# Seven block products of half-size matrices for the second half of an output projection's columns

## The reference

```python
hn   = rmsnorm(x, pre_gain)
q, k, v, g_a, u, g_b = split(hn @ w_in)          # 2048 -> 6 x 1024
y_a  = stick_breaking(q, k, v) * silu(g_a)       # 8 heads x 128
y_b  = multiscale_pool(u, w_pool) * silu(g_b)    # 4 groups x 256
mix  = concat(y_a, y_b)                          # 512 x 2048
out  = mix @ w_out                               # 2048 -> 2048
x    = x + rmsnorm(out, post_gain)               # norm over a token's 2048 columns
```

## Time and profile before

| | us |
|---|---|
| median of 3 runs | 749.54 (749.45 to 750.86) |
| profiled execution | 749.17 |
| its span | 747.4 |
| TensorE busy | 726.2 (97%), 3792 matmuls |
| VectorE busy | 527.9 (71%) |
| ScalarE busy | 406.0 (54%) |
| GpSimd busy | 62.8 (8%) |

### The profile page before, as it was taken

How to read it: one execution, slowest core, us unless ns; L and a number is a source line. 1 busy time by engine, 2 the same in 40 slices (tenths; PEclk the granted TensorE clock), 3 DMA queues, 4 the chain that set the end, 5 groups by cost and what they waited for, 6 DMA issues and landing times.

```text
span 747.4 us, 9753 instructions
## 1 busy us (share of the span) xinstructions
PE 726.2 (97%) x3792; PEld 618.4 (83%) x3792; DVE 527.9 (71%) x661; ACT 406.0 (54%) x538; POOL 62.8 (8%) x85
## 2 busy tenths in 40 slices
PE   6999989999999999999999999999999999999995
PEld 4778868888888888888888888888877888888884
DVE  3499978888788888788888987897978532133323
ACT  4754566666666656766657666756676232222200
POOL 0000000110020110020110011110000000000000
PEclk9999999999999999999999999999999999999998
DMA  8955445676646666746756656666644613053143
GB/s 288 390 152 129 139 109 146 168 176 171 173 107 178 170 165 182 175 114 169 193 147 169 173 150 170 169 148 163 181 140 172 225 62 138 26 169 102 67 142 112
DMA packets 36237, 118.08 MB, mean 158 GB/s; under 512 B 4064, under 2 KB 5088, under 8 KB 35552
## 3 DMA queue, kind: packets, MB, share of 16 engines
q1 hardware_dynamic: 30288, 96.49, 38.9%
q0 software_dynamic: 5760, 20.97, 16.5%
q10 hardware_dynamic: 144, 0.01, 0.0%
HBM read 113.26 MB, written 4.19 MB: 157 GB/s over the span
## 4 chain that ended last, share of the span: by engine, by line
PE 79%; DVE 9%; ACT 4%; issue 3%; DMA 2%; SPq 1%; POOL 0%; DVEq 0%; POOLq 0%; ACTq 0%
PE ps L1361 33%; PE ps L1363 17%; PE ps L1301 9%; PE ps L1300 9%; PE ps L1299 9%; DMA x_rows<-x 2%; DVE raw_lo L830 2%; DVE mix L867 1%; PE ps L1391 1%; PE ps L1389 1%; ACT w_hi L486 1%; DVE a_ops L899 1%; DVE a_ops L897 1%; DVE a_ops L1082 1%; SPq L381 0%
## 5 line engine op out<-in xcount | busy, mean ns | idle before, releaser
L1361 PE MATMUL ps<-a_ops,w_hi 128*128 128x512 f32 x1120 | 397.9, 399 | 3.6 <-ACT p_neg L584 1.6
L1363 PE MATMUL ps<-a_ops,raw_lo 128*128 128x256 f32 x1120 | 314.2, 281 | 0.0
L1361 PEld LDWEIGHTS ps<-a_ops,w_hi 128*128 128x128 f32 x1120 | 210.5, 188 | 55.8 <-DVE raw_lo L830 2.5
L830 DVE TENSOR_TENSOR raw_lo<-raw,w_hi 128x1024 fp32r<-128x1024 f32 x155 | 188.2, 1219 | 34.7 <-ACT w_hi L486 33.9
L1363 PEld LDWEIGHTS ps<-a_ops,raw_lo 128*128 128x128 f32 x1120 | 211.5, 189 | 0.3
L486 ACT ACTIVATE w_hi<-raw 128x1024 fp32r<-128x1024 f32 x155 | 163.3, 1055 | 66.4 <-PE ps L1363 62.9
L1299 PE MATMUL ps<-a_ops 128*128 128x512 f32 x192 | 75.0, 391 | 1.4 <-DVE a_ops L1082 1.1
L1300 PE MATMUL ps<-a_ops 128*128 128x512 f32 x192 | 74.8, 390 | 0.0
L1301 PE MATMUL ps<-a_ops 128*128 128x512 f32 x192 | 74.7, 389 | 0.0
L1270 POOL DMA_DIRECT2D raw<-w_heads x40 | 34.9, 871 | 308.4 <-DMA raw<-w_heads 308.4
L1090 DVE TENSOR_TENSOR a_ops<-raw,a_ops 128x1024 fp32r<-128x1024 f32 x24 | 28.3, 1219 | 37.8 <-ACT a_ops L682 37.8
(11 more groups left out here) (147 smaller groups left out, 919.5 us busy)
## 6 DMA issues: line engine op xcount, KB each, us to landing
raw<-w_heads SPq DMA_DIRECT2D x100, 512.0 KB, 4.9
raw<-w_heads POOLq DMA_DIRECT2D x40, 512.0 KB, 7.3
raw<-w_out SPq DMA_DIRECT2D x32, 512.0 KB, 4.5
raw<-w_v SPq DMA_DIRECT2D x15, 512.0 KB, 10.1
mix<-xT SPq DMA_DIRECT2D x16, 256.0 KB, 9.9
x_rows<-x SPq DMA_DIRECT2D x4, 1024.0 KB, 12.5
raw<-x SPq DMA_DIRECT2D x8, 512.0 KB, 5.2
out<-mix SPq DMA_DIRECT2D x6, 512.0 KB, 2.7
```

The costliest lines, as they stand in the source:

```text
L830: dve.tensor_tensor(raw_slot(raw_lo, slot), raw_slot(raw, slot), hi_slot(g).bitcast(F32), ALU.subtract).then_inc(w_split, 1)
L1361: pe.matmul(dst, hi[:, w], a_ops[:, a:a + SEQ], start=k == 0 and p in (0, 1, 5), stop=False, skip_group_check=True)
L1363: mm = pe.matmul(dst[:, HALF:SEQ], lo[:, w], a_ops[:, a:a + HALF], start=False, stop=k == KH - 1, skip_group_check=True)
```

## The change

The dc 0 quarter stays. The dc 1 quarter is computed with the same matmuls, but in eight "plain" steps of half a chunk (24 matmuls each) whose weights are rounded into the three slots of `w_hi` and subtracted into ten slots (`late_slot`), where the chunks had slots of their own. The two last quarters, dc 2 and 3 together, become one block product: tokens in halves of 256, inner dimension in halves of 1024, columns in halves of 512, and seven products of halves in place of eight. A product is 4 steps (q) of 2 inner tiles x 2 row tiles x 3 = 12 matmuls. The order of the steps is the list `LATE`. Weight t + 2 is rounded once step t - 1 is through (`late_hi_of` waits for `late_done >= t`).

For this, four operands of the mix tiles are new: three sums (`s_sums`, `s4_sums`, split by `s_hi_of`, `s_lo_of` into the places of the first three weight chunks) and one difference (split by `s3_hi_of`, `s3_lo_of` in place of mix parts that the plain steps have used). Of the weights, products 1 and 4 want the sum of two blocks (a load and an adding DMA by GpSimd, `add_late`), products 2 and 6 a sum of VectorE's (`late_sum`). The results are put together by ScalarE's copies out of PSUM (`keep_of`) and VectorE's sums (`join_e2`, `join_f`, `join_g`, `join_second`, `join_c12`). Rows 2 and 3 are complete after step 28 (of 0 to 35), rows 0 and 1 only behind the last two steps. The gain rows are loaded behind chunk 3 instead of before chunk 0. The rows are finished in the order 2, 3, 0, 1, and row 1 has the four pieces. Each square now waits for the one before it, since they share one scratch tile. In one tile (row 0, dc 3) the first token, whose mix is zero, is multiplied by 0 (`not_first`).

```diff
+PAIRS = KH // 2
+LATE = [("plain", q) for q in range(2 * PAIRS)]
+LATE += [(p, q) for q in range(PAIRS) for p in (0, 1, 2, 6)]
+LATE += [(3, 0)] + [(4, q) for q in range(PAIRS)] + [(3, q) for q in range(1, PAIRS)]
+LATE += [(5, q) for q in range(PAIRS)]
+LATE_STEPS = len(LATE)
+LATE_SLOTS = 10
+LATE_OF = {kind: t for t, kind in enumerate(LATE)}
+FORM = 2 * PAIRS
+ROW_ORDER = (2, 3, 0, 1)
+TAIL_ROWS = (0, 1)
...
+        FORM_BANK = {0: ACC, 5: ACC, 1: ACC + 2, 3: ACC + 2, 2: 0, 4: 0, 6: 2}
...
+        FORM_TILES = ((2, 2), (2, 3), (3, 2), (3, 3), (0, 3), (1, 3), (0, 2), (1, 2))
...
@@ SyncE
+            sp.wait_ge(o_chunk_done, KK)
             sp.dma_start(post_gain_rows[:, :],
                          post_gain.partition_broadcast(P)).then_inc(rows_gain_loaded, 16)
-            for j in range(RAW_SLOTS, OUT_HALVES + RAW_SLOTS):
-                sp.wait_ge(o_split, j - RAW_SLOTS + 1)
-                load_half(j)
+            load_late(RAW_SLOTS)
+            load_late(RAW_SLOTS + 1)
+            sp.wait_ge(s_split, 3 * PAIRS)
+            load_late(RAW_SLOTS + 2)
+            for t in range(LATE_SLOTS, LATE_STEPS + 2 * TT):
+                sp.wait_ge(late_done, t - LATE_SLOTS + 1)
+                load_late(t)
@@ ScalarE
+            for q in range(PAIRS):
+                s_hi_of(q, 1)
+                s_hi_of(q, 2)
+            for q in range(PAIRS):
+                s_hi_of(q, 3)
+                if q < 2:
+                    late_hi_of(q)
+            for t in range(LATE_STEPS - 2):
+                late_hi_of(t + 2)
+                if t == 0:
                     for s in range(TT):
-                        rows_square(s, n // KK)
+                        rows_square(s, 0)
+                if PAIRS <= t < 2 * PAIRS:
+                    s3_hi_of(t - PAIRS)
+                if t == FORM:
+                    for s in range(TT):
+                        rows_square(s, 1)
+                if t == LATE_OF[0, PAIRS - 1] + 1:
+                    keep_of(0, 0)
+                    keep_of(0, 1)
+                if t == LATE_OF[1, PAIRS - 1] + 1:
+                    keep_of(1, 0)
+                    keep_of(1, 1)
+                if t == LATE_OF[4, PAIRS - 1] + 1:
+                    for n in range(4):
+                        rows_square(*FORM_TILES[n])
+            for n in range(4, 8):
+                rows_square(*FORM_TILES[n])
@@ VectorE
+            for q in range(PAIRS):
+                s_sums(q)
+                s_lo_of(q, 1)
+                s_lo_of(q, 2)
+            for q in range(PAIRS):
+                s4_sums(q)
+                s_lo_of(q, 3)
+                if q < 2:
+                    late_lo_of(q)
             dve.wait_ge(rows_gain_loaded, 16)
+            for t in range(LATE_STEPS - 2):
+                if LATE[t + 2][0] == 1:
+                    late_sum(2, LATE[t + 2][1])
+                if LATE[t + 2][0] == 2:
+                    late_sum(6, LATE[t + 2][1])
+                late_lo_of(t + 2)
...
+                if t == LATE_OF[2, PAIRS - 1] + 1:
+                    join_e2(0)
+                    join_e2(1)
+                if t == LATE_OF[6, PAIRS - 1] + 1:
+                    join_f(0)
+                    join_f(1)
+                    join_g(0)
+                    join_g(1)
+                if t == LATE_OF[4, PAIRS - 1] + 1:
+                    join_second(0)
+                    join_second(1)
+                if t == LATE_OF[4, PAIRS - 1] + 2:
+                    for n in range(4):
+                        rows_gain(*FORM_TILES[n])
+                if t == LATE_OF[4, PAIRS - 1] + 3:
+                    row_mean(2)
+                    row_mean(3)
+                if t == LATE_OF[3, PAIRS - 1] + 1:
+                    join_c12(0)
+                    join_c12(1)
...
+            row_final(2)
+            for i in range(2):
+                rows_gain(i, 3)
+            row_final(3)
+            for n, s in enumerate(TAIL_ROWS):
...
+                rows_gain(s, 2)
+                row_final(s)
@@ GpSimd
+            for q in range(PAIRS):
+                add_late(1, q)
+            for q in range(PAIRS):
+                add_late(4, q)
@@ TensorE
+            def form_tile(t, i):
+                p, q = LATE[t]
+                for k in range(2):
+                    mm = three(form_bank(p, i), form_operand(p, 2 * q + k, i), late_weights(t, k),
+                               p in (0, 1, 2, 4, 6) and q == 0 and k == 0,
+                               p in (3, 4, 5, 6) and q == PAIRS - 1 and k == 1)
+                return mm
...
+            for t in range(FORM):
+                plain_step(t)
+            for t in range(FORM, LATE_STEPS - 2):
+                form_step(t)
+            t = LATE_STEPS - 2
+            pe.wait_ge(late_split, t + 1)
+            form_tile(t, 0)
+            pe.wait_ge(late_split, t + 2)
+            form_tile(t + 1, 0).then_inc(c11_done, 1)
+            form_tile(t, 1)
+            form_tile(t + 1, 1).then_inc(c11_done, 1)
```

More of the change, by code:

```diff
@@ L99, in slot_turns @@
             lands((u, p), ROLE[u][p])
-    for j in range(OUT_HALVES + ROW_HALVES):
+    for j in range(OUT_HALVES):
         lands(("half", j), half_slot(j))
+    for t in range(LATE_STEPS + 2 * TT):
+        lands(("late", t), late_slot(t))
     return turn
@@ L128, in hybrid_layer @@
             raw_lo = sb("raw_lo", [P, RAW_SLOTS * QUARTER], F32R, heads)
-            post_gain_rows = sb("post_gain_rows", [P, D], scope=heads)
         sb("raw_kept", [P, RAW_SLOTS * QUARTER])
+        with ExitStack() as outs:
+            sb("w_hi_pad", [P, (HI_SLOTS - 1) * QUARTER], scope=outs)
+            o_sum = [sb(f"o_sum{i}", [P, SEQ], scope=outs) for i in range(2)]
         w_hi = sb("w_hi", [P, HI_SLOTS * QUARTER], F32R)
@@ L159, in hybrid_layer @@
             o_lo3 = sb("o_lo3", [P, CHUNK], F32R, outs)
+        with ExitStack() as outs:
+            post_gain_rows = sb("post_gain_rows", [P, D], scope=outs)
+            with ExitStack() as more:
+                raw_more = sb("raw_more", [P, 2 * QUARTER], scope=more)
+            raw_more_lo = sb("raw_more_lo", [P, 2 * QUARTER], F32R, outs)
         with ExitStack() as heads:
@@ L289, in hybrid_layer @@
         final_done = sem("final_done")
+        s_summed = sem("s_summed")
+        s_hi_done = sem("s_hi_done")
+        s_split = sem("s_split")
+        s3_hi_done = sem("s3_hi_done")
+        s3_split = sem("s3_split")
+        late_hi_done = sem("late_hi_done")
+        late_split = sem("late_split")
+        late_done = sem("late_done")
+        late_summed = sem("late_summed")
+        late_t1 = [sem(f"late_t1_{q}") for q in range(PAIRS)]
+        late_t3 = [sem(f"late_t3_{q}") for q in range(PAIRS)]
+        kept = sem("kept")
+        joined = sem("joined")
+        c11_done = sem("c11_done")
         POOL_CONSTS = 4
@@ L809, in _ @@
-            o_hi_of(OUT_CHUNKS - 1)
-            for s in range(TT):
-                rows_square(s, TT - 1)
+                at = ss_at(s, dc)
+                junk = work[:, :]
+                if (s, dc) == (0, 3):
+                    act.activation(junk, src, ACT.Square, scale=not_first[:, 0:1],
+                                   accum_out=out_ss[:, at:at + 1]).then_inc(rows_squared, 1)
+                else:
+                    act.activation(junk, src, ACT.Square,
+                                   accum_out=out_ss[:, at:at + 1]).then_inc(rows_squared, 1)
@@ new lines, in row_final @@
+            def row_final(s):
+                n = ROW_ORDER.index(s)
+                for dc in range(TT):
+                    dve.wait_ge(rows_free, rows_count(s, dc))
+                dve.wait_ge(out_rstd_ready, n + 1)
+                for a, b in final_pieces(s):
+                    t = LATE_STEPS + 2 * n + a // QUARTER
+                    dve.wait_ge(raw_loaded[late_slot(t)], TURN["late", t])
+                    rows = rows_part(s, a, b)
+                    dve.scalar_tensor_tensor(rows, rows, out_rstd[:, s:s + 1],
+                                             late_raw(t)[:, a % QUARTER:a % QUARTER + b - a],
+                                             ALU.mult, ALU.add).then_inc(final_done, 1)
@@ new lines, in plain_step @@
+            def plain_step(t):
+                q = LATE[t][1]
+                pe.wait_ge(late_split, t + 1)
+                for s in range(TT):
+                    if t == 0 and s == Y:
+                        pe.wait_ge(y_free, HEADS)
+                    for k in range(2):
+                        tile = 2 * q + k
+                        mm = three(rows_bank(1, s),
+                                   both((mix_part(tile, 0), mix_part(tile, 1)), s * P, (s + 1) * P),
+                                   late_weights(t, k), t == 0 and k == 0, t == FORM - 1 and k == 1)
+                    if t == FORM - 1 and s < TT - 1:
+                        mm.then_inc(rows_done, 1)
+                mm.then_inc(late_done, 1)
```

351 lines of the change are left out of this document (273 added, 78 removed).

## The result

The changed kernel takes 741.35 us (740.5 to 741.8, 4 runs) against 750.2 (749.45 to 750.98, 4 runs) of the kernel before: a ratio of 0.9877, 95% interval 0.9858 to 0.9896, so 1.2% faster. The direction was right, the size was not: 8.85 us between the medians, 7.4 between the profiled spans, where I had given it 4.8. The profiled execution took 741.75 us with a span of 740.0.

The account below looks back on a forecast made before the run. TensorE bounds the projection, VectorE's chain its end: 10.96 us saved, 1.2 back as waits, 4.9 as longer end, so 4.8 less, span 742.6; plus 1.77 around it and 0.37 to the median, 744.8 us predicted; range 742.6 to 748.6.

Parts of the forecast that it names:

- The step that failed: Stages ahead of the output projection: read only the projection's windows, since the diff touches nothing before it; late work starts at 607.9.
- TensorE's share: Last 1024 output columns: 336 matmuls for 384 at 0.2284 us, 10.96 us less, 1.2 given back as waits.
- The start: First late steps: mix sums, splits and gain rows hidden beside matmuls, third weight 2.9 us to spare, no cost.
- The transfers: Steps 25 to 28: four adding DMAs want 12.3 us of the engines beside plain loads; cost taken as 0.
- my limit: Last weight needing an adding DMA: must stand by 701.1, or 704.1 us with the 3 us to spare.
- my 57.6%: Adding queue's share of the engines while both queues had packets; the last adding DMA lands at 701.4 us.
- by a half: Strict half share of the engines for the adding queue: last lands at 704.6, 0.5 us too late; not added.
- The end: Behind the last matmul: VectorE without rest, last final ends 739.4, 9.7 us from last matmul instead of 4.5; span 742.6.
- (a): Rival for the projection: the whole 10.96 us arrive, end no longer than before, 738.6 us; 4%.
- (b): Rival: adding transfers late by 0.5 to 6 us, or gain rows by 3, TensorE waits mid-projection: 745.5 to 748; 15%.
- (c): Rival: slower; four adding transfers one after another at 9.2 us, TensorE stops 10.7 us at step 28: 755.5; 7%.
- (d): Rival: VectorE later still in the end, 0.1 us more at each of some 25 hand-offs: 747.3; 8%.

Follow-up runs that it names:

- before_pad32: The kernel before with one unused tile of 32 bytes per partition behind out_rstd, where the change put not_first: 746.69 us, ratio 0.9963.
- after_nf_mid: The changed kernel with not_first last and a 32-byte pad ahead of tri_lo, moving attention's and pooling's tiles but not x_hi, x_lo: 741.42 us.
- after_nf_last: The changed kernel with not_first allocated last, so all other tiles stand where they stood before the change: 744.31 us, ratio 0.9930.
- last_add_twice: The changed kernel with the last adding DMA (product 4's fourth weight) issued a second time once it has landed: 746.86 us, ratio 0.9961.

## Why the prediction missed

**The step that failed** is its first: "Then the windows of the output projection, because the diff touches nothing before it." I took from this that the time ahead of the projection stays as it is. The diff touches no instruction there, but one 32-byte tile moves operands of the earlier stages. In its place the runs show -2.33 us of span in the two profiles and -2.9 in the times (before_pad32 against before, and after_nf_mid against after_nf_last, each pair on one chip). The profiles are one execution each: in kernels with the changed placement their late step 0 lies anywhere between 603.97 and 605.55 us. Of the 3.45 us between 744.8 and 741.35, 2.33 are this, 0.27 the late part, and 0.8 that the profiled execution lay 0.37 below its median before and 0.4 above it after, which is chance from run to run. I had no term for the placement, and I see nothing in the trace of before from which its sign could be read; it could only have widened the range, to below 742.

**TensorE's share was right.** 336 matmuls for 384, forecast -10.0 us by the prediction's own times (739.7 to 729.7), measured -9.94. (Its closing sum writes 10.96 - 1.2, which is 9.8, and a longer end of 4.9 where its times give 5.2; both come to 4.8.) I had one spacing, 0.2284 us, which is a mean of unequal chunks. In the changed kernel it is 0.231 to 0.232 in steps 7 to 9, 17 to 19 and 27 to 29, whose lo parts stand in the three moved slots (raw_more, raw_last), and 0.2267 in the others without a wait (0.2277 in step 0). The waits of steps 31 to 33 came to 1.4 us (0.43, 0.82 and 0.18 over 2.72).

**The start had its cover.** Sums, splits and the third weight stood at 611.8 (610.57 + 1.22), 4.7 us ahead of step 2's first matmul at 616.46; the gain rows landed in 4.5 us, not 6.6.

**The transfers.** The last adding DMA was issued at 688.99 and landed 10.9 us later, at 699.9, 1.9 us before my limit moved by 2.33. The queues from 680 to 700 us, which hold all packets of the four adding transfers (576, at 144 each):

```profile
q0 software_dynamic: 576, 2.10, 54.4%
q1 hardware_dynamic: 940, 3.43, 44.3%
...
raw_more<-w_out POOLq DMA_DIRECT2D x2, 512.0 KB, 9.7
```

They took 54.4% of the engines over 20 us, 10.9 us of all 16 where I had summed 12.3. By my 57.6% the last would have landed at 699.1, by a half at 702.3, so my bound was the nearer one. The Trainium skill ("DMA: Bandwidth & Descriptors", SWDGE vs HWDGE vs iDMA) has each engine go round-robin between the queues of the two kinds. Over these 20 us the trace agrees roughly, 54.4% against 44.3%; from 682 to 684 us the adding queue had 98.0% against 2.2%.

**The end** was forecast 12.9 us long behind the last matmul and is 12.59, with VectorE's chain as worked out. Rivals: (a), the whole 10.96 us, did not come, though the time lies 3 us from it; (b), (c) and (d) did not happen, and last_add_twice shows what a late adding transfer would have looked like.

## What to carry to other kernels

Sum the engine that will be the last one, not the one that is busiest: here TensorE lost 9.9 us and VectorE's end gave half of it back, to 0.3 us as summed from rows. Give a range room for placement: whatever allocates or frees a tile moves all tiles behind it, and 32 bytes were worth over half of what the rewrite itself gave (2.9 us beside 5.3); when the part that the change doesn't touch moves in the trace, pad the old kernel before looking for a reason in the new one. Before taking work off VectorE, see whether GpSimd would stand in its way and whether the stores behind it can start sooner.

## What I had not expected of the hardware

The spacing of a stream of matmuls at the full granted clock has two values, 347 and 353 ns for a pair of 512 and 256 columns, and a stream kept the lower one for up to 24 groups of 16. Where other tiles stand in SBUF changes how often it has which: 32 or 64 bytes for q, k, tri and the rest turned 9 or 13 fast groups of 140 into 70 and more. Where a matmul's own weights stand matters too: 0.2333 us in one place, 0.2267 in one 64 bytes further on.
